# Two branch projections taken as three products of rounded halves, with a new order of the small work on the other engines

## The reference, cut to what matters

```python
hn = rms_norm(h, attn_norm[l])
p = hn @ w_in[l]
rq, rk, rv, rg, pw, qa, kva, gl = jnp.split(p, IN_SPLITS, axis=-1)
y_ret = retention_mix(rq, rk, rv, rg, cos_ret, sin_ret)          # 512 wide
y_rwkv = rwkv7_mix(pw, ...)                                      # 512 wide
y_mla = mla_mix(qa, kva, ...)                                    # 512 wide, "latent"
ys = jnp.stack([y_ret, y_rwkv, y_mla], axis=2)
branch = jnp.einsum('bsnc,ncd->bsnd', ys, w_branch[l])           # three 512 x 1024 products
gates = jax.nn.sigmoid(gl.reshape(B, S, N_BRANCH, D_MODEL))
merged = jnp.sum(gates * branch, axis=2)
h = h + merged @ w_o[l]
hn = rms_norm(h, ffn_norm[l])
h = h + (swiglu(hn, ...) if l % 2 == 0 else moe_swiglu(hn, ...)) # layer 1: 2 of 8 experts
```

## Time and profile before

| | |
|---|---|
| median of three runs | 1674.45 us (1673.33 to 1675.45) |
| the profiled execution | 1675.91 us, its span 1674.1 us |
| TensorE busy | 1615.5 us (97%) in 15502 records |
| VectorE, ScalarE, GpSimd busy | 649.5, 441.7, 175.0 us |
| chain that ended last, by engine | PE 82%, DMA 10%, DVE 5%, ACT 2% |
| the same, by line | L1458 30%, L2119 and L2138 (experts) 37%, waits for expert weights 9%, L1690 4% |

### The profile page before, as it was taken

How to read it: one execution, slowest core, us unless ns; L and a number is a source line. 1 busy time by engine, 2 the same in 40 slices (tenths; PEclk the granted TensorE clock), 3 DMA queues, 4 the chain that set the end, 5 groups by cost and what they waited for, 6 DMA issues and landing times.

```text
span 1674.1 us, 34454 instructions
## 1 busy us (share of the span) xinstructions
PE 1615.5 (97%) x15502; PEld 1002.9 (60%) x15502; DVE 649.5 (39%) x1077; ACT 441.7 (26%) x652; POOL 175.0 (10%) x172
## 2 busy tenths in 40 slices
PE   8999999999999999999999999989999799999996
PEld 7877767788888877776754336343462334634433
DVE  6679757655555669757532010000100001000012
ACT  5576423454344566523310000000000000000001
POOL 1264102200000075100300000000000000000010
PEclk9999999999999999999999999999999999999999
DMA  9745223555445752212899999999999999999996
GB/s 342 241 148 172 97 72 130 212 201 188 170 171 199 227 185 103 101 52 102 331 425 429 426 429 429 428 428 429 429 428 429 430 428 429 429 428 419 406 430 256
DMA packets 85113, 494.26 MB, mean 295 GB/s; under 512 B 5560, under 2 KB 14644, under 8 KB 61752
## 3 DMA queue, kind: packets, MB, share of 16 engines
q1 hardware_dynamic: 80224, 480.65, 71.2%
q0 software_dynamic: 2064, 7.67, 1.2%
q10 hardware_dynamic: 2680, 3.74, 0.7%
HBM read 484.91 MB, written 6.16 MB: 293 GB/s over the span
## 4 chain that ended last, share of the span: by engine, by line
PE 82%; DMA 10%; DVE 5%; ACT 2%; issue 0%; SPq 0%; DVEq 0%; ACTq 0%
PE bank L1458 30%; PE bank L2119 26%; PE bank L2138 11%; DMA slot<-moe_units_dram 9%; PE bank L1690 4%; PE bank L1450 2%; PE bank L1665 2%; PE bank L2081 1%; PE bank L2053 1%; DVE ring_lo L2182 1%; PE bank L1724 1%; DVE tmp L2182 0%; DMA h<-x_dram 0%; PE bank L2043 0%; PE bank L1479 0%; PE bank L1615 0%
## 5 line engine op out<-in xcount | busy, mean ns | idle before, releaser
L2119 PE MATMUL bank<-slot,xg 128*32 128x512 f32 (+1 forms) x5120 | 488.4, 539 | 9.0 <-DMA slot<-moe_units_dram 8.7
L2119 PEld LDWEIGHTS bank<-slot,xg 128*32 128x32 f32 x5120 | 169.6, 110 | 312.5 <-issue 276.6
L2138 PE MATMUL bank<-slot,ehT 128*32 128x256 f32 x4480 | 252.5, 383 | 24.7 <-DMA slot<-moe_units_dram 23.7
L2138 PEld LDWEIGHTS bank<-slot,ehT 128*32 128x32 f32 x4480 | 144.3, 111 | 128.0 <-DMA slot<-moe_units_dram 32.1
L2182 DVE TENSOR_TENSOR ehm<-bank,esg 128x512 f32<-128x512 f32 (+3 forms) x32 | 23.7, 741 | 466.1 <-ACT esg L1360 466.1
L1360 ACT ACTIVATE esg<-bank 128x512 f32<-128x512 f32 (+3 forms) x32 | 20.4, 637 | 491.2 <-PE bank L2119 491.2
L2182 DVE TENSOR_TENSOR ring_lo<-ring,i_hi 128x2048 fp32r<-128x2048 f32 (+2 forms) x36 | 80.4, 2240 | 62.1 <-ACT i_hi L1025 62.1
L2971 DVE COPY ehT<-bank 128x512 f32<-128x512 f32 (+3 forms) x32 | 23.7, 742 | 205.5 <-PE bank L2081 205.5
L2182 DVE TENSOR_TENSOR ring_lo<-ring,f_hi 128x2048 fp32r<-128x2048 f32 (+1 forms) x36 | 75.4, 2112 | 63.4 <-ACT f_hi L1287 63.4
L1458 PE MATMUL bank<-i_hi,ix_hi 128*128 128x512 f32 (+1 forms) x256 | 98.6, 385 | 0.6 <-DVE ring_lo L2182 0.6
L1458 PE MATMUL bank<-i_hi,ix_lo 128*128 128x512 f32 (+1 forms) x256 | 98.5, 385 | 0.0
(11 more groups left out here) (490 smaller groups left out, 2218.7 us busy)
## 6 DMA issues: line engine op xcount, KB each, us to landing
slot<-moe_units_dram SPq DMA_DIRECT2D x166, 2048.0 KB, 29.4
ring<-w_in_dram SPq DMA_DIRECT2D x25, 2048.0 KB, 8.8
ring<-w_branch_dram SPq DMA_DIRECT2D x6, 2048.0 KB, 7.9
ring<-ffn_w_gate_dram SPq DMA_DIRECT2D x5, 2048.0 KB, 7.9
ring<-ffn_w_up_dram SPq DMA_DIRECT2D x5, 2048.0 KB, 7.8
ring<-ffn_w_down_dram SPq DMA_DIRECT2D x5, 2048.0 KB, 7.9
ring<-w_o_dram SPq DMA_DIRECT2D x2, 2048.0 KB, 9.0
ring<-w_o_dram SPq DMA_DIRECT2D x4, 1024.0 KB, 6.2
```

The source lines that it names most:

```text
L2119: ins = M(psum[GROUP * p:GROUP * p + GROUP, to:to + width], xg[:, x, o:o + GROUP], w[:, c, p, :], start=x == 0 and to % 512 == 0, stop=x = ...
L2138: ins = M(psum[GROUP * p:GROUP * p + GROUP, o:o + 256], ehT[:, x, GROUP * i:GROUP * i + GROUP], w[:, c, p, :], start=x == 0 and o % 512 == ...
```

## The change

Retention and latent branch now go by `branch_step`: eight steps for each branch, and in a step one chunk of 128 rows by 512 columns for both token tiles, six fp32r matmuls. ScalarE writes the high half of each weight chunk (`branch_high`, six buffers `b_hi`), GpSimd the low half. ScalarE reads a turned y out twice, once rounded (`yT`) and once whole (`y_of`), and GpSimd subtracts (`y_low`). The eight steps of retention lie in tile 0, the eight of the latent branch in tile 1; the retention y is turned and read out a head earlier (i = 7); `Z` is computed before the levels; gate units move. VectorE scales the retention result in four pieces in the heads 3 to 6 instead of two whole passes in the heads 1 and 2, and takes `g_low(1)` and `g_low(3)` earlier. The load of the final norm's gain moves to the middle of layer 1. The experts' down product writes 512 columns at once for the first two groups of an item, in another layout of `ey`; the last item keeps its old form.

```diff
+            def branch_step(i):
+                n, u, c, _, _, lo, hi = b_step(l, i)
...
+                pe.wait_ge(s.y_lo_ready, 8 * l + Y_LOW.index((n, c)) + 1)
+                pe.wait_ge(s.b_lo_ready, 16 * l + i + 1)
+                for t in range(T):
...
+                    for k, (x, w) in enumerate(((y, hi[:]), (y, lo), (yT_lo[n][c][:, tok], hi[:]))):
+                        ins = M(dst[:], x, w, start=c + k == 0, stop=c == 3 and k == 2, skip_group_check=True)
@@ TensorE, tile t
-                branch(0, ret_slot, t, t)
+                for i in range(4):
+                    branch_step(8 * t + i)
                 if t == 0:
                     latent_values(3)
-                gate_units(*((48, 50), (70, 72))[t])
...
-                gate_units(*((50, 64), (72, 80))[t])
+                gate_units(*((48, 64), (68, 80))[t])
+                branch_step(8 * t + 4)
...
                 if t == 0:
-                    gate_units(66, 68)
+                    gate_units(64, 65)
                     read_out(pe, f"U0.{l}")
                     state_sum(0)
-                    branch(0, ret_slot, 1, 0)
+                    gate_units(65, 66)
                     correction(1)
-                    mla_slot = branch_slot(2)
-                    branch(2, mla_slot, 0, 0)
                     read_out(pe, f"dU11.{l}")
                     state_sum(1)
@@ ScalarE
+            def branch_high(i):
+                _, _, _, m, w, _, hi = b_step(l, i)
...
+                own.step(A.activation(hi[:], w, ACT.Copy), s.b_hi_ready)
...
+                copy_out(f"Z{t}.{l}", zz[:])
                 if t:
                     g_high(20)
                     g_high(21)
                 else:
+                    branch_high(6)
+                    branch_high(7)
                     g_high(18)
...
                 for n in (22, 23) if t else (19,):
                     g_high(n)
+                for i in () if t else (8, 9, 10, 11):
+                    branch_high(i)
@@ GpSimd
+                if n in (12, 14, 15):
+                    y_low((12, 14, 15).index(n))
+            for i in range(16):
+                if i < 4:
+                    y_low(3 + i)
+                if i == 4:
+                    y_low(7)
+                _, _, _, _, w, lo, hi = b_step(l, i)
+                pool.wait_ge(s.b_hi_ready, 16 * l + i + 1)
+                G.tensor_tensor(lo, w, hi[:].bitcast(F32), ALU.subtract).then_inc(s.b_lo_ready, 1)
@@ VectorE
-                if i == 1:
-                    group_scale(y_ret[:], 0, P, 3 * l)
                 if i == 2:
+                    dve.wait_ge(s.gn_root_ready, 3 * l + 1)
+                    step(V.reciprocal(stat[:, 4, 0:8], stat[:, 4, 0:8]))
+                if i == 3:
                     dve.wait_ge(s.silu_g_ready, l + 1)
-                    step(tt(y_ret[:], y_ret[:], raw[:, 3, :, :], ALU.mult), s.ret_done)
+                if 2 < i < 7:
+                    finish_retention(i - 3)
```

More of the change, by code:

```diff
@@ L492, in build @@
     y_rwkv = sb("y_rwkv", [P, T, W], where=hn_at)
+    qa_at = at[0]
     qa = sb("qa", [P, T, MLAC])
@@ L736, in glus, with down_parts, ey_free @@
         eng.wait_ge(s.glu_ready, pair * 8 + (n + 1))
-    def ey_free(eng, pair, j):
-        eng.wait_ge(s.ey_stored, pair * 128 + (64 * j + 16))
+    def down_parts(j, k, last=False):
+        if j and last:
+            return [[(GROUP * p, g, 1536 + 512 * g, 256 * p, 256) for p in range(4)] for g in range(2)]
+        parts = [(GROUP * (2 * g + c), g, 1536 * j, 512 * c, 512) for g in range(2) for c in range(2)]
+        return [parts] + [[(GROUP * p, 2, 1536 * j + 512, 256 * p, 256) for p in range(4)]] * (GROUPS[k] > 2)
+    def ey_free(eng, pair, j, last):
+        eng.wait_ge(s.ey_stored, pair * 192 + ((128 if last else 64) * j + 16))
     def panel_loaded(n):
@@ L1170, in latent_out, with retention_out @@
             def latent_out(k):
-                copy_out(f"oP{k}.{l}", yT[2][:, k, :], SEQ)
+                b = product(act, f"oP{k}.{l}")
+                own.step(A.activation(yT[2][:, k, :], b[:, 0:SEQ], ACT.Copy))
+                own.free(A.activation(y_of[2][k][:], b[:, 0:SEQ], ACT.Copy), f"oP{k}.{l}")
+            def retention_out(u):
+                b = product(act, f"yT0{u}.{l}")
+                own.step(A.activation(yT[0][:, 2 * u:2 * u + 2, :], b[:].rearrange("p (c n) -> p c n", c=2), ACT.Copy))
+                for i in range(2):
+                    ins = A.activation(y_of[0][2 * u + i][:], b[:, SEQ * i:SEQ * i + SEQ], ACT.Copy)
+                    own.free(ins, f"yT0{u}.{l}") if i else own.step(ins)
+            def branch_high(i):
+                _, _, _, m, w, _, hi = b_step(l, i)
+                if i % 8 == 0:
+                    act.wait_ge(slot_loaded[m % RING], panel_loaded(m))
+                if i in (4, 5) or i > 7:
+                    b_step_used(act, l, i - 2 if i < 8 else i - 4)
+                own.step(A.activation(hi[:], w, ACT.Copy), s.b_hi_ready)
             def probs_out(i):
@@ L1234, in _ @@
                     probs_out(NH - 1)
-                for u in range(2 if t == 0 else 0):
-                    copy_out(f"yT0{u}.{l}", yT[0][:, 2 * u:2 * u + 2, :])
-                if t == 0:
+                    branch_high(2)
+                    branch_high(3)
                     latent_out(3)
@@ L1245, in _ @@
                     g_high(17)
+                for i in (12, 13, 14, 15) if t else (4, 5):
+                    branch_high(i)
                 gate(6 + 2 * t)
@@ L1638, in latent_values, with turn_retention @@
                 done(ins)
+            def turn_retention():
+                pe.wait_ge(s.ret_done, l + 1)
+                for u in range(2):
+                    b = bank(f"yT0{u}.{l}")
+                    for i in range(2):
+                        for t in range(T):
+                            ins = TR(b[:, 256 * i + 128 * t:256 * i + 128 * t + 128], y_ret[:, t, 2 * u + i:W:4], ident)
+                    done(ins)
             for i in range(NH + 1):
@@ L1738, in _ @@
                     done(ins)
-                branch_part(*dealt, 1, 2)
+                branch_step(8 * t + 5)
+                vcol = pr[:, t, 1024:1536]
+                b = bank(f"Z{t}.{l}")
+                for i in range(NH):
+                    hh = slice(64 * i, 64 * i + 64)
+                    ins = by_chunk(b, hh, m1[:, 4 * (i % 2) + i // 2, 128:192], vcol[:, hh])
+                done(ins)
                 for lv in range(LEVELS):
@@ L2410, in scale_probs, with finish_retention @@
                          s.scaled_ready if t else None)
+            def finish_retention(hd):
+                cols = slice(P * hd, P * hd + P)
+                for t in range(T):
+                    step(V.scalar_tensor_tensor(out=y_ret[:, t, cols], in0=y_ret[:, t, cols],
+                                                scalar=stat[:, 4, 4 * t + hd:4 * t + hd + 1], in1=raw[:, 3, t, cols],
+                                                op0=ALU.mult, op1=ALU.mult), s.ret_done if t and hd == RH - 1 else None)
             for i in range(NH):
@@ L2557, in _ @@
                 if t:
-                    step(add_gated(2, 1, 0))
+                    for i in range(T):
+                        step(add_sigs(0, i))
                     add_bonus()
@@ L2577, in _ @@
                                     ALU.add), f"{name}{t}{lv}{g}.{l}")
+                for i in range(T):
+                    gated(2 * t, 1, i)
                 if t:
                     g_low(20)
-                    step(add_gated(2, 0, 1))
                     g_low(21)
                     turned_low(0)
-                else:
-                    g_low(17)
-                    gated(0, 0, 1)
                 for n in (2 * t, 2 * t + 1):
@@ L2602, in _ @@
                     if n == 3:
-                        step(add_gated(2, 1, 1))
+                        for i in range(T):
+                            step(add_sigs(1, i))
                     if n < 3:
```

180 lines of the change are left out of this document (90 added, 90 removed).

## The result

The changed kernel takes 1714.35 us (median of 4 runs, 1712.15 to 1716.59), the kernel before on the same chip 1674.48 (1673.33 to 1675.45): 1.0238 times the time, 95% interval 1.0226 to 1.025. It is 39.9 us slower. My sum had +14.5, and the range went up to 1702: right in sign, 25 us short.

What follows compares the result with a forecast made beforehand. TensorE's chain was taken to bound the mixers, transfers at some 428 GB/s the rest. Gains of 20.7 us against losses of 17.6 a layer, 35.2, made +14.5: 1690.4, as a median 1689 us, range 1667 to 1702.

Steps and rivals of the forecast that it cites:

- Quarter 19, the term that decides: Tile 1, ahead of the pair products: TensorE stands 4.3 us behind ScalarE's queue; +6.5 us a layer, bounds 4.3 and 8.
- the second solve: Tile 1's 15 short steps: GpSimd's low halves of steps 12 to 15 fall there; +2 us a layer, bounds 0.3 and 4.2.
- the products' gain: Retention and latent products in both mixers: fp32r steps replace float32 matmuls; -6.7 us a layer, -13.4 us.
- My four terms (3, 1.6, 2 and 1): GpSimd's losses a layer, in us: low halves against `rows_of`, step 6, the second solve, the k halves.
- step 6: After `Z`, TensorE waits for step 6's copies and GpSimd's low half; +1.6 us a layer, bounds 0 and 1.7.
- The k halves: From 283.1 us they come at GpSimd's pace, the fourth about 2 us late; +1 us a layer, bounds 0 and 2.
- Rival (4), the port: Second solve and elsewhere: every GpSimd subtraction halts VectorE in full; 1702 us, chance 0.12.
- VectorE's order: Head loop: moved `y_ret` pieces and earlier `g_low(1)` shorten TensorE's waits; -2.3 us a layer, -4.6.
- the gain's load: 512 KB leave the stretch that the transfers bound; -1.2 us, bounds 0 and -1.2.
- the slow lot of rows 7: Layer 0, twelve matmuls after the wait for `sm` in 4.21 instead of 2.75 us; its going gives -1.5 us.
- ScalarE's copies: More copies on the chain ahead of the first pair products; +2.3 us a layer, bounds 1.5 and 2.8.

Runs made afterwards that it cites:

- e16: The kernel before with the second of four matmuls left out of each of the eight retention and latent products per layer: 1665.19 us.
- e17: e13 with the third matmul of each triple (low half of y with the weights' high half) left out: 1667.53 us.
- e13: e4 with GpSimd's subtractions for the low parts of branch weights, k halves and y replaced by two memsets each: 1675.87 us.
- e4: The changed kernel with gate units 66 and 67 in tile 0, b_hi 8 to 11 behind tile 1's tT copies, latent sums behind tile 1's end: 1694.39 us.
- e9: The kernel before with the change's other order of VectorE alone: 1672.23 us, ratio 0.9988.
- e8: The kernel before with the change's down product and load of the final gain alone: 1673.95 us, ratio 1.0.
- e5: e4 with ScalarE making the k halves' high parts earlier, ahead of g_hi 22 and g_hi 23: 1706.97 us.
- e7: The changed kernel with GpSimd's 16 branch weight subtractions per layer replaced by two memsets each: 1701.87 us.
- e2: The changed kernel with ScalarE's b_hi 8 to 11 made behind tile 1's tT copies: 1705.30 us.
- e11: Units and sums as in e4, but VectorE makes the 16 branch weight low parts per layer and ScalarE's high halves are moved to suit: 1706.99 us.
- e14: e4 with ScalarE making b_hi 6 and 7 ahead of the Z copy: 1692.57 us.
- e1: The changed kernel with gate units 66 and 67 issued in tile 0 again: 1700.82 us.
- e3: The changed kernel with the two latent sums on VectorE behind the end of tile 1: 1712.92 us.

## Why the prediction was right or wrong

By the table, my sum missed 12.4 of the 19.3 us in layer 0, and twice that is about the whole miss. It lies line by line: 1.8 up to the first products with `rows_of`, 2.6 in the rest of tile 0 (1.5 of it Y at half pace, 0.8 the wait for the gates), 5.4 at quarter 19's place, 0.4 in the second solve, and 2.2 behind it.

**The step that failed most: the size of "Quarter 19, the term that decides".** Its mechanism is right. ScalarE's queue is as described, and TensorE waits 4.2 us for `tT` where I had 4.3. But I took +6.5 a layer and the table has +11.9, since I left everything behind that wait at the prices of before. The variance was halted by 2 us beside GpSimd's subtractions, so TensorE stood another 2.8 us for `m`. I had priced halts only for `rows_of` and the solve. And the 24 matmuls of steps 8 to 11 took 8.09 us for 5.46; the slow clock stood in the upper bound alone. By the runs, giving the two units back gains 6.8 a layer, and with the copies and the sums moved as well it is 10.0, clock included.

**One microsecond for one: the products' gain.** "-13.4 us" rests on my sentence that in the mixers "each microsecond of TensorE work or waiting counts one to one". By e16 and e17 some 57% do (40 to 76%), which would make 7.6 us of the 13.4 (an estimate, that the share holds here too). I had named the exception myself, VectorE's solve of tile 1 "just ahead of TensorE", and yet took the gain there in full. The runs of 3.63 us taken out elsewhere did count: in e13, where the halts are gone, the stretch from the first state product to the end of tile 0 is 3.0 us shorter, and the one ahead of the last transposes of `y_rwkv` 3.5.

**GpSimd, too small and partly in the wrong places.** My four terms (3, 1.6, 2 and 1) made 7.6 a layer, the memsets give 4.3 + 1.8 + 3.2 = 9.3 on top of e4. Two were right: from the last pair products of tile 0 to `rows_of` the changed kernel needs 10.2 us for 7.0 (I had +3), and step 6 waits 1.7. The k halves were late as I said (TensorE waited 1.7 us for them), but off the chain; on it they halted tile 1's variance: 2.82 for 0.70. In the second solve four multiplications stretch by 0.8 each, 3.2 in all, of which the shift between the third and fourth lines of the table shows 2.4; I had 2. Rival (4), the port, at 1702, was right in kind: its sign that the short multiplications "stretch beyond 1 us each four times" came almost to the letter (1.06, 1.00, 0.99, 0.98). It did not decide alone. Of the 40 us, e4 gives back 20.0 and the memsets on top of it 18.5, but the first part holds the variance's halts and some 8 us of slow clock beside the queue, the second some faster supply beside the halts.

**VectorE's order and the gain's load.** -4.6 was -2.3, the clock's -1.5 in it not seen; the load's -1.2 can't be told from nothing. I had read VectorE waiting for TensorE in the heads 3 to 6; in the changed kernel the `y_ret` pieces there stand on the chain of waits (166.81, 172.51 and 176.26). The wait for `sm` of 1.8 us went from its head and came back, spread over two (2.3 us in the changed kernel, 1.5 in e9), because the pieces take 1.86 us for two beside GpSimd's cast and low part, and 0.60 without. And the slow lot of rows 7 was not bound to that wait. In e8, with the same head loop and the same wait of 1.8, the next twelve matmuls take 2.75 us, and the clock from 120 to 180 us is 1.00, not 0.97:

```profile
120.00:180.00 60.00, 57.08 (x302) 44.41 (x301) 56.05 (x104) 37.31 (x81) 28.92 (x25) 1.00 0.43 152
```

**What the runs leave open, and what a trace says of it.** e13 has the units and copies moved and none of these subtractions left, and is still 2.2 us above the kernel before. TensorE's waits in its layer 0 (120 to 345 us) add up to 10.9 us, before to 3.6: +7.3, against -6.7 of its own work. Among them:

```profile
PE bank L1777 <- POOL ring_lo L1006: 1.8, 2, 1.5
PE bank L1777 <- ACT sig L1217: 1.6, 2, 0.8
PE bank L1710 <- ACT y L1237: 1.4, 2, 1.0
PE bank L1793 <- DVE m L2254: 1.3, 1, 1.3
```

The first is mostly step 6 and the third ScalarE's second copies of y. With them the last pair products of tile 0 start at 189.05, in e9 at 186.30: 2.75 us for ScalarE's copies, where I had 2.3. The second stands in no term of mine: the gate units now come directly ahead of steps 4 and 12, which wait for the gates. That makes 3.2 us in both layers. No run took these waits out one by one, so their prices are read from the trace and not shown by an experiment.

## What to carry to other kernels

When a term says that an engine will stand still, price what comes behind the wait anew: here the wait itself was right to 0.1 us, and the work behind it was 5 us dearer a layer than at its old prices. A cheaper product on the engine that looks busiest is worth only what the chain beside it leaves: take a quarter of it out as a trial before pricing its replacement, and look at what the removed work stood in front of. Work moved to an idle engine is not free: here GpSimd's subtractions held the VectorE instructions with two SBUF operands that stood beside them, so their price is read from VectorE's timeline at that time, and moving them can just move the victim (e5). In an in-order queue, a copy that waits for a buffer belongs behind the copies that another engine is waiting for.

## What was not expected of the hardware

- GpSimd's reading, not its being busy, halts VectorE: beside subtractions of 1.25 us four multiplications of 0.2 us took 0.98 to 1.06, beside pairs of memsets of 1.05 us 0.19 to 0.22 (e7).
- Not only two-operand instructions are held: in e2 and e4 the copies `pairs` (one SBUF operand, four in 2.12 us, 1.24 in e11) and in e4 a scaling of eight columns were held by GpSimd's subtractions. A reduction that stood ahead of it kept its 0.69 us:

```profile
243.95 0.69 DVE L2287 TENSOR_REDUCE stat<-kk 128x8 f32<-128x512 f32 x1
244.67 0.74 DVE L2289 TENSOR_SCALAR stat<-stat 128x8 f32<-128x8 f32 x1
```

```profile
244.12 5.00 POOL L1002 TENSOR_TENSOR ring_lo<-ring,b_hi 128x512 fp32r<-128x512 f32 x4 [20.96 <-ACT b_hi L1241]
```

- GpSimd is held in turn: four k subtractions took 11.44 us in e5 beside dense VectorE work, 9.80 in e4.
- The clock did not follow one wait by a rule. In the changed kernel Y of tile 0 ran at half pace at 237.7 to 240.7, behind waits of TensorE of 1.7 us (up to 222.11) and 1.0 (up to 236.31). In e2 the same two waits stand there, and Y of layer 0 ran at full pace. Behind a wait of 1.9 us for `m` the 24 matmuls of steps 8 to 11 took 6.91 us in e14 and were not slow in e4. Behind waits of 4.1 to 4.3 they were slow in all four kernels that had one (8.09, 7.92 in e1, 7.74 in e3, 7.22 in e7).
